# Gated delta rule heads loop: output gate read from PSUM, mask added by TensorE, lower triangle made by GpSimd

## The chip, the cores and the metric

The kernel runs on one core of a Trainium2 chip. The metric is the device time of one execution in microseconds (us), here the median of three runs. All numbers on single instructions come from one further execution that the hardware profiler recorded.

## The reference

The network has three layers on 256 tokens of width 1024: a gated delta rule (GDN) layer, a forgetting attention layer, and a block of windowed attention, pooling and an expert product over 16,384 experts. Only the GDN layer is touched. It has 8 query and key heads and 16 value heads of size 128; its projection also gives an output gate z. In the reference the chunks have 64 tokens; cut to what matters:

```python
g = cumsum(g)                                     # log decay within a chunk
decay = exp(where(lower, g[:, None] - g[None, :], -inf))
L = where(strict, (k * beta) @ k.T * decay, 0.0)
T = inverse(eye + L)                              # unit lower triangular
u, w = T @ (v * beta), T @ (k * beta * exp(g))
attn = (q @ k.T) * decay
# along the chunks
v_new = u - w @ state
o = (q * exp(g)) @ state + attn @ v_new
state = state * exp(g_last) + (k * exp(g_last - g)).T @ v_new
# behind it
o = rmsnorm(o, norm_w) * silu(z)
```

The second layer's input is scaled and shifted by a modulation vector, cond @ ada_w[1], of which the GDN layer's loop computes the first 2048 entries beside its own work.

## The kernel before, in words

Each engine has one instruction stream, written out by hand; semaphores order them against each other. No planner is used. A helper's call order in a stream is the order of its work.

The heads loop is `rounds(inner)`, eight rounds, each for one key head and its two value heads (g is 0 or 1), with the 256 tokens as two chunks of 128. Three rounds are in work at once: in round i the triangular inverse of head pair i is built (`level_p`, `mask_level`, `level_d`, `close_level`, j = 0 to 5), the pair before, f, is finished (`finish`, steps 0 to 5: values, state, second chunk, output, sum of squares), and the next pair, n, is set up. Round 0 has no f and round 7 no n. A level is a ping-pong: TensorE's product into bank PA, a masking copy by VectorE, TensorE's product into bank PB, and VectorE's subtraction from the inverse. The finish and setup products stand between the levels on TensorE in the order of `inner`.

Setup of pair n: `setup_keys` makes K K^T and K Q^T in PSUM; `setup_rows` (L2372) spreads the cumulative log decay and beta over 128 partitions into the PSUM banks ROWS; ScalarE takes EG = exp of a row (L931); VectorE adds the mask negu (`decays`, L1623) into the SBUF tile DT, ScalarE takes the exponential of DT in place (L937), VectorE multiplies beta and K K^T (`betas`, L1632) and then that and DT into the lower triangle LT (`lowers`, L1638); `setup_values` (L2393) transposes V into ROWS, and `setup_low` (L2402) gathers the diagonal blocks of LT, from which `starts` begins the next inverse. GpSimd makes the masked scores AT (L680) and the decayed queries (L683).

Output of pair f: ScalarE copies o to OS and squares it; TensorE sums the squares (L2494); ScalarE makes 1/rms (L986, L988); VectorE's `normed` multiplies OS with the norm weight and 1/rms (L1689) and then with the gate (L1692).

Modulation: SyncE loads 1 MB of ada_w[1] a round (L533), GpSimd multiplies eight slices with cond (L691) and adds them in seven additions (L696), TensorE sums over partitions with two products of one column (`modulator`, L2410), VectorE copies the result (L1696). SyncE starts the load for round i when TensorE's modulation product of round i - 2 is done; GpSimd does the slices of round i before the scores of pair i + 1.

`norm_sums` (L2356) sums squares of q and k for the pair after next. Around the loop stand the input projection before (L2253), with `setup_*` of round 0 between its last tiles, and the output projection behind it (L2551), between whose products the last `finish` stands.

## Time and profile before

| | |
|---|---|
| median of 3 runs | 1618.76 us (1617.99 to 1621.35) |
| profiled execution | 1621.4 us, its span 1619.6 us |
| TensorE (PE) busy | 1554.8 us, 96% |
| VectorE (DVE) busy | 1109.9 us, 69% |
| ScalarE (ACT) busy | 932.7 us, 58% |
| GpSimd (POOL) busy | 493.4 us, 30% |
| DMA | 255.89 MB, mean 158 GB/s |
| mean granted TensorE clock | 0.987 |

The span runs from the first to the last instruction. PE is TensorE's matmuls, PEld its weight loads, SPq SyncE's queue of DMAs. An fp32 product stands in the trace as two records, so "x4" of a shape is two products, except for transposes. A matmul's length holds a latency that overlaps the next one; the distance between starts is what it takes of the engine. "[0.67 <-PE ps L2372]" is idle time before the row and the instruction that ended it.

### The profile page before, as it was taken

The page shows a single profiled execution, that of the slowest core. Times are in us where ns is not written, and L with a number is a line of the kernel's source. Part 1 is how long each engine was busy: PE and PEld are TensorE (multiplying, and loading weights), DVE is VectorE, ACT ScalarE, POOL GpSimd, SP SyncE. Part 2 cuts the span into 40 slices and gives each one's busy share as a digit, 9 for nine tenths or more (in the row PEclk, how much of TensorE's full clock was granted, in tenths as well). Part 3 has the DMA queues.
Part 4 walks back from the last instruction along what each step waited for, and adds up shares of the span by engine and source line. Part 5 has one row for each costly group of instructions (what it writes and reads, how often), then busy time and mean ns, then how long its engine had stood idle before and what let it go on. Part 6 is the DMA issues. An engine that isn't in the chain of part 4 may idle for free.

```text
span 1619.6 us, 37025 instructions
## 1 busy us (share of the span) xinstructions
PE 1554.8 (96%) x13269; PEld 1429.3 (88%) x13269; DVE 1109.9 (69%) x2304; ACT 932.7 (58%) x1763; POOL 493.4 (30%) x405
## 2 busy tenths in 40 slices
PE   7899999899999999999999999999999999999998
PEld 6899877798998899888999999999999888888886
DVE  3787768656556653776478888798888555555554
ACT  1766567744555555545354444799898544555554
POOL 4000278661000040000067777766565100000000
PEclk9999979899999999999999999999999999999999
DMA  9668412454443344247455555544444666666663
GB/s 295 219 184 278 150 55 82 133 163 130 151 131 118 111 156 131 79 157 156 104 150 167 168 168 172 162 143 135 140 131 143 182 194 194 193 192 190 194 193 127
DMA packets 211832, 255.89 MB, mean 158 GB/s; under 512 B 15912, under 2 KB 193804, under 8 KB 211724
## 3 DMA queue, kind: packets, MB, share of 16 engines
q1 hardware_dynamic: 211723, 254.39, 53.2%
q8 instruction: 76, 1.25, 0.3%
q14 instruction: 33, 0.26, 0.1%
HBM read 253.29 MB, written 1.05 MB: 157 GB/s over the span
## 4 chain that ended last, share of the span: by engine, by line
PE 72%; DVE 11%; issue 5%; DMA 4%; ACT 4%; SPq 2%; DVEq 0%; ACTq 0%
PE ps L2253 22%; PE ps L2861 22%; PE ps L2843 10%; PE ps L2831 3%; DMA raw<-in_u_experts 3%; PE ps L2273 2%; PE ps L2551 2%; DVE raw L2014 2%; SPq L580 2%; PE ps L2628 1%; DVE w_lo L1396 1%; PE ps L2451 1%; DMA arena<-in_ada_w 1%; DVE arena L2067 1%; PE ps L2648 1%
## 5 line engine op out<-in xcount | busy, mean ns | idle before, releaser
L742 POOL TENSOR_TENSOR w_lo<-raw,w_hi 128x1024 fp32r<-128x1024 f32 x128 | 307.6, 2406 | 337.7 <-ACT w_hi L1265 337.6
L2253 PE MATMUL ps<-x_hi,w_hi 128*128 128x256 f32 x1088 | 315.3, 290 | 8.3 <-DVE w_lo L1396 3.0
L2253 PE MATMUL ps<-x_hi,w_lo 128*128 128x256 f32 x1088 | 308.2, 283 | 0.0
L2253 PE MATMUL ps<-x_lo,w_hi 128*128 128x256 f32 x1088 | 308.2, 283 | 0.0
L2212 DVE TENSOR_TENSOR w_lo<-raw,w_hi 128x1024 fp32r<-128x1024 f32 x124 | 152.0, 1226 | 143.2 <-ACT w_hi L1374 143.2
L1374 ACT ACTIVATE w_hi<-raw 128x1024 fp32r<-128x1024 f32 x124 | 131.6, 1061 | 168.0 <-PE ps L2861 168.0
L2253 PEld LDWEIGHTS ps<-x_hi,w_hi 128*128 128x128 f32 x1088 | 209.1, 192 | 15.3 <-issue 6.0
L2253 PEld LDWEIGHTS ps<-x_lo,w_hi 128*128 128x128 f32 x1088 | 209.2, 192 | 1.3 <-issue 1.2
L2253 PEld LDWEIGHTS ps<-x_hi,w_lo 128*128 128x128 f32 x1088 | 209.0, 192 | 0.0
L1265 ACT ACTIVATE w_hi<-raw 128x1024 fp32r<-128x1024 f32 x128 | 134.9, 1054 | 113.4 <-DVE raw L2014 113.2
L2806 PE MATMUL ps<-x_hi,w_hi 128*128 128x256 f32 x576 | 166.3, 289 | 10.6 <-ACT arena L1287 9.7
L2014 DVE STREAM_TRANSPOSE raw<-raw 128x1024 f32<-128x1024 f32 x128 | 158.3, 1237 | 17.1 <-DMA raw<-in_u_experts 15.8
L2806 PE MATMUL ps<-x_lo,w_hi 128*128 128x256 f32 x576 | 162.8, 283 | 0.0
L2806 PE MATMUL ps<-x_hi,w_lo 128*128 128x256 f32 x576 | 162.7, 282 | 0.0
L2861 PE MATMUL ps<-w_hi,x_hi 128*128 128x512 f32 x512 | 157.6, 389 | 1.1 <-DVE x_lo L2202 1.1
L2861 PE MATMUL ps<-w_lo,x_hi 128*128 128x512 f32 x512 | 157.7, 389 | 0.0
L2861 PE MATMUL ps<-w_hi,x_lo 128*128 128x512 f32 x512 | 157.6, 389 | 0.0
L1396 DVE TENSOR_TENSOR w_lo<-arena,w_hi 128x2048 fp32r<-128x2048 f32 (+1 forms) x43 | 97.1, 2258 | 70.0 <-ACT w_hi L759 70.0
L1396 DVE TENSOR_TENSOR w_lo<-raw,w_hi 128x2048 fp32r<-128x2048 f32 (+1 forms) x43 | 97.2, 2261 | 69.3 <-ACT w_hi L759 69.3
L2843 PE MATMUL ps<-x_lo,w_hi 128*128 128x256 f32 x448 | 131.9, 294 | 0.0
L2843 PE MATMUL ps<-x_hi,w_hi 128*128 128x256 f32 x448 | 126.7, 283 | 0.0
L2843 PE MATMUL ps<-x_hi,w_lo 128*128 128x256 f32 x448 | 126.5, 282 | 0.0
(446 smaller groups left out, 3563.7 us busy)
## 6 DMA issues: line engine op xcount, KB each, us to landing
raw<-in_u_experts SPq DMA_DIRECT2D x512, 128.0 KB, 2.7
raw<-in_v_experts SPq DMA_DIRECT2D x128, 512.0 KB, 4.3
arena<-in_ada_w SPq DMA_DIRECT2D x18, 1024.0 KB, 7.8
raw<-in_a_w_in SPq DMA_DIRECT2D x12, 1024.0 KB, 5.7
arena<-in_a_w_in SPq DMA_DIRECT2D x12, 1024.0 KB, 5.7
raw<-in_b_w_in SPq DMA_DIRECT2D x8, 1024.0 KB, 5.7
arena<-in_b_w_in SPq DMA_DIRECT2D x8, 1024.0 KB, 5.6
raw<-in_w_in SPq DMA_DIRECT2D x8, 1024.0 KB, 5.6
```

What stands on the lines that cost most here:

```text
L580: sp.dma_start(URAW[u][32 * q:32 * q + 32, :].rearrange("p (a c) -> p a c", a=4), src).then_inc(u_in[u], 16)
L742: pool.tensor_tensor(UTL[e], UT[e % 2], UTH[e].bitcast(F32), ALU.subtract).then_inc(utl_ready, 1)
L1265: act.activation(UTH[e % 4], UT[e % 2], ACT.Copy).then_inc(uth_ready, 1)
L1374: act.activation(VH[u], VRAW[u], ACT.Copy).then_inc(high_ready, 1)
L1396: v.tensor_tensor(WLO[:, slot, 0:k, :], RAW[raw_slot(base, u)][:, 0:k, :], WHI[:, slot, 0:k, :].bitcast(F32), ALU.subtract).then_inc(lo_re ...
L2014: v.transpose(UT[s_].rearrange("p (k a j) -> p a k j", k=KC, a=4), URAW[s_].rearrange("p (a k i) -> p a k i", a=4, k=KC)).then_inc(ut_read ...
L2212: v.tensor_tensor(VL[u], VRAW[u], VH[u].bitcast(F32), ALU.subtract).then_inc(low_ready, 1)
L2253: ins = mm(o[:, b * S:b * S + S], w[:, slot, kk, b * P:b * P + P], xx[:, (kk + turn) % KC, :], start=(kk == 0 and n == 0), stop=(kk == k - ...
L2806: ins = mm(ps[e % 2][:, 0:S], w[e % 4][:, kk * P:kk * P + P], xx[:, kk, :], start=(kk == 0 and n == 0), stop=(kk == KC - 1 and n == 2))
L2831: ins = mm(GB.rearrange("p (e t) -> p t e", t=4)[:, q, :], OHJ[:, c % 2, q, :], OHI[:, c % 2, q, :], start=True, stop=True, skip_group_che ...
L2843: ins = mm(ps[e % 2][:, 0:S], w[e % 4][:, kk * P:kk * P + P], xx[:, kk, :], start=m == 0, stop=m == 23)
L2861: ins = mm(ps[4 + 2 * t + h][:, :], g[:, u, t * P:t * P + P], w[u][:, 512 * h:512 * h + 512], start=False, stop=False, skip_group_check=True)
```

## The change

TensorE adds the mask negu, now bf16, to ROWS with `ident16` (`setup_masks`); `decays` goes, and ScalarE's exponential reads ROWS in PSUM and writes DT. `lowers` moves from VectorE to GpSimd, ahead of its scores. The copy of o to OS goes: VectorE's `gated` multiplies o from PSUM, the norm weight and z in place, and `normed` multiplies that with 1/rms. The modulation product moves from the end of round i to behind `setup_values` of round i + 1, has four products instead of two, and GpSimd has one addition fewer. `keep_wide` puts products of 512 bf16 columns, whose result nobody reads, ahead of some levels. The order of several steps in `inner` changes on all three engines: on TensorE `level_d(i, 1)` goes ahead of `setup_keys` and `norm_sums` ahead of `level_p(i, 5)`; on VectorE `betas` goes ahead of `close_level(i, 2)`; on ScalarE `setup_v` goes ahead of the first two `spread`.

```diff
 RNo = [temp(256)]
-negu = temp(128)
+negu = temp(64).bitcast(B16)
+temp(64)
 strict = temp(128)
...
+    def lowers(r):
+        for g in range(2):
+            pool.wait_ge(h_dt, r.nth(g, 2))
+            pool.wait_ge(h_xm, r.nth(g))
+            pool.tensor_tensor(LT[r.side][g], KKb[g], DT[g], ALU.mult).then_inc(h_lt, 1)
...
     def scores(r):
+        lowers(r)
         pool.wait_ge(g_kqs, r.count(1, 1))
...
                                ALU.mult).then_inc(mod_sum, 1)
-        for half, done in ((4, 8), (2, 12), (1, 14)):
+        for half, done in ((4, 8), (2, 12)):
             pool.wait_ge(mod_sum, 15 * i + (24 + done))
             for kk in range(half):
-                pool.tensor_tensor(w[:, kk, :], w[:, kk, :], w[:, kk + half, :], ALU.add).then_inc(mod_sum, 1)
+                pool.tensor_tensor(w[:, kk, :], w[:, kk, :], w[:, kk + half, :], ALU.add).then_inc(mod_sum, half if half == 2 and kk else 1)
         if i + 1 < GQ:
...
     def setup_decays(r):
+        if r.at:
+            act.wait_ge(h_kd, r.count(2))
+            act.wait_ge(h_at, r.count(2))
+            act.wait_ge(h_lt, r.count(2))
         for g in range(2):
...
             for cc in range(2):
-                act.activation(two(DT[g])[:, cc, :], two(DT[g])[:, cc, :], ACT.Exp,
+                act.activation(two(DT[g])[:, cc, :], ROWS[g][:, cc * 128:cc * 128 + 128], ACT.Exp,
                                bias=NGT[:, cc, r.heads[g]:r.heads[g] + 1]).then_inc(h_dt, 1)
...
-    def finish_out(r):
+    def finish_squares(r):
+        for g in range(2):
+            act.wait_ge(h_o, r.nth(g))
+            act.activation(SQo[g], A2[g], ACT.Square).then_inc(h_sq, 1)
...
+    def finish_norms(r):
         if r.at:
             act.wait_ge(h_out, r.count(2, 2))
-        for g in range(2):
-            act.wait_ge(h_o, r.nth(g))
-            act.activation(OS[g], A2[g], ACT.Copy).then_inc(h_os, 1)
-            act.activation(SQo[g], A2[g], ACT.Square).then_inc(h_sq, 1)
...
-    def finish_norms(r):
         for g in range(2):
...
         if f:
-            finish_out(f)
+            finish_squares(f)
+        if n:
+            setup_v(n)
         spread(i, 0)
         spread(i, 1)
-        if n:
-            setup_v(n)
         spread(i, 2)
...
     finish_second(Round(GQ - 1))
-    finish_out(Round(GQ - 1))
+    finish_squares(Round(GQ - 1))
     finish_norms(Round(GQ - 1))
...
-    def decays(r):
-        if r.at:
-            v.wait_ge(h_kd, r.count(2))
-            v.wait_ge(h_at, r.count(2))
-        for g in range(2):
-            v.wait_ge(h_eg, r.nth(g))
-            v.tensor_tensor(two(DT[g]), two(ROWS[g][:, 0:256]), bcast(negu, 2), ALU.add).then_inc(h_dta, 1)
...
     def keys(r):
...
         for g in range(2):
+            v.wait_ge(h_eg, r.nth(g))
             v.tensor_tensor(two(KKb[g]), two(ROWS[g][:, 256:512]), KKs, ALU.mult).then_inc(h_xm, 1)
...
-    def lowers(r):
-        for g in range(2):
-            v.wait_ge(h_dt, r.nth(g, 2))
-            v.wait_ge(h_xm, r.nth(g))
-            v.tensor_tensor(LT[r.side][g], KKb[g], DT[g], ALU.mult).then_inc(h_lt, 1)
...
-    def normed(r, g):
+    def gated(r):
         if r.at >= 6:
             v.wait_ge(z_late, 1)
+        for g in range(2):
+            v.wait_ge(h_sq, r.nth(g))
+            zb = ZB[:, r.heads[g], :]
+            v.scalar_tensor_tensor(zb, A2[g], COLS[:, CAN:CAN + 1], zb, ALU.mult, ALU.mult).then_inc(h_os, 1)
...
+    def normed(r, g):
         v.wait_ge(h_orn, r.nth(g))
         v.wait_ge(h_os, r.nth(g))
-        v.scalar_tensor_tensor(OS[g], OS[g], COLS[:, CAN:CAN + 1], RNo[g], ALU.mult, ALU.mult).then_inc(h_og, 1)
-        v.wait_ge(h_og, r.nth(g, 1, 1, 2))
         zb = ZB[:, r.heads[g], :]
-        v.tensor_tensor(zb, OS[g], zb, ALU.mult).then_inc(h_out, 1)
+        v.tensor_tensor(zb, zb, RNo[g], ALU.mult).then_inc(h_out, 1)
...
         close_level(i, 0)
+        mask_level(i, 1)
         if ahead:
             normalised_k(ahead)
-        mask_level(i, 1)
         if f and f.at:
...
             remainder(f)
-        close_level(i, 2)
         if n:
-            decays(n)
+            betas(n)
         else:
             split_x_half(1, 0, ZB[:, 0:8, :])
+        close_level(i, 2)
         mask_level(i, 3)
-        if n:
-            betas(n)
+        if n is None:
+            split_x_half(1, 1, ZB[:, 0:8, :])
         close_level(i, 3)
         mask_level(i, 4)
-        if n:
-            lowers(n)
-        else:
-            split_x_half(1, 1, ZB[:, 0:8, :])
+        if f:
+            modulator(f)
+            gated(f)
         close_level(i, 4)
...
         mask_level(i, 5)
-        modulator(i)
         if f:
...
     lo(T_AIN + 16, 0, 8)
-    decays(Round(0))
     betas(Round(0))
-    lowers(Round(0))
     v.memset(XPAIR[0:32, :, 32:64], 0.0)
...
     normed(Round(GQ - 2), 1)
+    modulator(Round(GQ - 1))
     remainder(Round(GQ - 1))
+    gated(Round(GQ - 1))
     for g in range(2):
...
         pe.wait_ge(g_norm, r.count(2, 2))
-        pe.wait_ge(ada_free, r.count(1, 9))
+        pe.wait_ge(ada_free, r.count(1, 8))
         if r.at == 0:
...
-    def setup_values(r):
+    def setup_masks(r):
         for g in range(2):
...
             pe.wait_ge(h_xm, r.nth(g))
+            for cc in range(2):
+                ins = mm(ROWS[g][:, cc * 128:cc * 128 + 128], ident16, negu, start=False, stop=True, skip_group_check=True)
+            ins.then_inc(h_dta, 1)
...
+    def setup_values(r):
+        for g in range(2):
+            pe.wait_ge(h_dt, r.nth(g, 2))
             for cc in range(2):
...
         for cc in range(2):
-            ins = mm(MODP[:, cc:cc + 1], RAW[MOD_SLOT[r.side]][:, 0, cc * 128:cc * 128 + 128], ones[:, 0:1], start=True, stop=True)
+            for half in range(2):
+                ins = mm(MODP[:, cc:cc + 1], RAW[MOD_SLOT[r.side]][:, half, cc * 128:cc * 128 + 128], ones[:, 0:1],
+                         start=(half == 0), stop=(half == 1))
         ins.then_inc(raw_free, 1)
...
-    def level_p(r, j):
+    def keep_wide(bank_, n):
+        for _ in range(n):
+            mm(bank_[:, :], ident16, BG3, start=True, stop=True)
...
+    def level_p(r, j, spare=0):
         lt = LT[r.side]
+        keep_wide(PA, spare)
         if j == 0:
...
-    def level_d(r, j):
+    def level_d(r, j, spare=0):
+        if j == 0 and r.at:
+            pe.wait_ge(h_xx, r.count(12))
+        keep_wide(PB, spare)
         pe.wait_ge(h_pm, r.count(6, j + 1))
...
             pe.wait_ge(h_xt, r.count(3, 3))
-            if r.at:
-                pe.wait_ge(h_xx, r.count(12))
         elif j < 5:
...
             elif step == 3:
-                pe.wait_ge(h_og, r.nth(g, 1, 0, 2))
+                pe.wait_ge(h_og, r.nth(g))
                 mm(B2[g][:, 128:256], INVT[r.side][:, 2 * g + 1, :], R1[g], start=True, stop=True).then_inc(h_s3, 1)
...
                 pe.wait_ge(h_sq, r.nth(g))
+                pe.wait_ge(h_os, r.nth(g))
                 mm(B2[g], ones, SQo[g], start=True, stop=True).then_inc(h_oss, 1)
...
         level_p(i, 0)
-        level_d(i, 0)
+        level_d(i, 0, 2)
         if f:
             finish(f, 0)
-        level_p(i, 1)
+        level_p(i, 1, 0 if f else 2)
         if f:
             finish(f, 1)
+        level_d(i, 1, 0 if f else 2)
         if n:
             setup_keys(n)
-        level_d(i, 1)
+        level_p(i, 2, 0 if n else 1)
         if f:
             finish(f, 2)
-        level_p(i, 2)
         if n:
             setup_rows(n)
-        level_d(i, 2)
+        level_d(i, 2, 0 if n else 1)
         if f:
             finish(f, 3)
+        if n:
+            setup_masks(n)
         level_p(i, 3)
...
             finish(f, 4)
-        level_d(i, 3)
+        level_d(i, 3, 0 if f else 2)
         if n:
             setup_values(n)
-        level_p(i, 4)
-        level_d(i, 4)
+        if f:
+            modulator(f)
+        level_p(i, 4, 0 if n else 2)
+        level_d(i, 4, 1)
         if f:
...
             setup_low(n)
-        level_p(i, 5)
-        modulator(i)
         if i.at + 2 < GQ:
             norm_sums(Round(i.at + 2))
+        level_p(i, 5, 0 if f else 2)
         level_d(i, 5)
...
     pe.wait_ge(cv_out, 16)
+    setup_masks(Round(0))
     setup_values(Round(0))
...
         finish(Round(GQ - 1), step)
+        if step == 1:
+            modulator(Round(GQ - 1))
     for u in range(1, 4):
         pe.wait_ge(lo_ready, tile_no(T_AOUT, 0, u))
+        if u == 2:
+            pe.wait_ge(ada_free, 10 + GQ)
         if u < 3:
...
         else:
```

## Rows read from the trace of the kernel before

**Rows 1.** The page, part 4: shares of the last chain by engine.

```profile
PE 72%; DVE 11%; issue 5%; DMA 4%; ACT 4%; SPq 2%; DVEq 0%; ACTq 0%
```

**Rows 2.** By stretch: us, busy (count) of each engine, granted clock, DMA share, GB/s.

```profile
196.30:203.30 7.00, 4.80 (x235) 3.56 (x235) 3.73 (x15) 2.12 (x9) 6.84 (x12) 0.99 0.02 5
203.30:220.30 17.00, 15.33 (x277) 12.07 (x278) 8.16 (x24) 7.63 (x26) 14.15 (x22) 0.50 0.21 64
...
230.90:246.20 15.30, 14.36 (x401) 11.21 (x400) 13.02 (x38) 11.77 (x39) 13.15 (x20) 1.00 0.22 71
...
309.10:322.70 13.60, 11.95 (x252) 10.14 (x252) 5.62 (x17) 7.64 (x15) 6.26 (x9) 0.50 0.76 241
```

**Rows 3.** Timeline of round 2, TensorE: start, length, engine, line, shapes, count.

```profile
230.86 0.45 PE L2424 MATMUL ps<-arena 32*32 32x32 f32 x32
...
233.84 0.61 PE L2381 MATMUL ps<-arena 128*128 128x128 f32 x4
...
234.94 0.44 PE L2451 MATMUL ps<-arena 32*32 32x16 f32 x32
...
236.39 0.60 PE L2372 MATMUL ps<-arena,small 128*128 128x512 bf16 x2
...
238.32 0.49 PE L2489 MATMUL ps<-arena 128*128 128x128 f32 x2
...
240.23 0.66 PE L2393 MATMUL ps<-small,arena 128*128 128x128 f32 x4
...
240.81 0.44 PE L2429 MATMUL ps<-arena 32*32 32x32 f32 x16
...
242.03 1.13 PE L2494 MATMUL ps<-arena,small 128*128 128x256 f32 x4
...
243.09 0.45 PE L2402 MATMUL ps<-small,arena 32*32 32x32 f32 x32
...
244.07 0.61 PE L2410 MATMUL ps<-small,arena 128*128 128x1 f32 x4
...
244.54 1.10 PE L2356 MATMUL ps<-arena,small 128*128 128x512 f32 x2
...
245.58 0.67 PE L2462 MATMUL ps<-arena 64*64 64x64 f32 x8
...
246.18 0.45 PE L2424 MATMUL ps<-arena 32*32 32x32 f32 x32
```

**Rows 4.** Timeline of round 2, ScalarE and VectorE.

```profile
236.88 0.45 ACT L931 ACTIVATE arena<-ps 128x128 f32<-128x128 f32 x2 [0.67 <-PE ps L2372]
...
237.44 0.22 DVE L1664 TENSOR_TENSOR arena<-arena,ps 128x64 f32<-128x64 f32 x1 [0.22 <-PE ps L2451]
...
241.51 1.25 DVE L1638 TENSOR_TENSOR arena<-arena 128x256 f32<-128x256 f32 x2
...
244.90 0.43 DVE L1658 COPY arena<-ps 64x256 f32<-64x256 f32 x1
```

**Rows 5.** Timeline of GpSimd, rounds 1 and 2, and the landing of L533's DMAs.

```profile
232.46 5.69 POOL L696 TENSOR_TENSOR arena<-arena 128x256 f32<-128x256 f32 x7
...
240.06 1.41 POOL L680 TENSOR_TENSOR arena<-arena 128x256 f32<-128x256 f32 x2 [1.92 <-PE ps L2491]
...
242.44 4.69 POOL L691 TENSOR_TENSOR raw<-raw,small 128x256 f32<-128x256 f32 x7
...
DMA to landing us min/median/max: 5.0/5.3/7.8
```

**Rows 6.** Timeline, TensorE: projection's end, start of rounds 1 and 7, last finish.

```profile
194.10 0.60 PE L2393 MATMUL ps<-small,arena 128*128 128x128 f32 x4
...
213.03 0.65 PE L2424 MATMUL ps<-arena 32*32 32x32 f32 x32
...
308.42 0.45 PE L2424 MATMUL ps<-arena 32*32 32x32 f32 x32
...
327.95 0.69 PE L2474 MATMUL ps<-arena 128*128 128x128 f32 x4 [0.86 <-issue]
```

## The prediction

> **What bounds the kernel now.** I read the page's chain of waits first: 72% of the span is TensorE, so what counts is TensorE's order of work [rows 1]. Only the heads loop, between 196 and 328 us, and its two neighbours are edited, so the next view is the busy time and granted clock by stretch. Two stretches, 17.0 and 13.6 us long, were granted 0.50 of the clock, which is the 1.2 GHz level; both come just after stretches in which TensorE had many short pauses (before the first, 4.80 us busy of 7.00). A steady round has the full 2.4 GHz and TensorE 14.36 us busy of 15.30 [rows 2]. The third view is TensorE's timeline of one steady round: from the first level product (230.86) to the next round's (246.18) it takes 15.32 us [rows 3]. Start-to-start distances there are the prices of blocks of products. VectorE, ScalarE and GpSimd are read beside it [rows 4, 5].
>
> In such a round the chain alternates between TensorE (level products) and VectorE (masks, closings). At 235 TensorE does the key products ahead of the level-1 product. Around 238.3 it does the twelve output passes (L2489 to L2491) ahead of the level-3 closing product. From 241.5 VectorE does the two lower-triangle products, 1.25 us, and only then closes level 4. From 243.1 to 246.2 TensorE is all but closed up: 0.98 for the low blocks and level 5, 0.47 for the modulation product, 1.04 for the norm sums, 0.60 for the closing [rows 3, 4].
>
> **The change, part by part, in a steady round.** I count from the first level product as 0.
>
> *Start.* Two wide products stand before the level-0 closing. One wide bf16 product costs 0.21 (two of the same shape, L2372, show 0.60 with 0.2 of latency in it [rows 3]), so 0.43. They start only after VectorE's last closing, which comes at about 0.55, so the closing product starts at about 1.05, where it now starts at about 1.0. Cost 0.1.
>
> *Level 1.* The key products move behind the level-1 closing product. They take 1.1 (233.84 to 234.94 [rows 3]), and VectorE's late output gate is one operation instead of two (0.7 less). Level 1 closes 0.65 earlier, at 3.95. The keys then end at 4.45, and the row products start at about 5.3 instead of 5.53.
>
> *Betas.* They now stand before the level-2 closing on VectorE, and wait for ScalarE's exponentials, which start 0.49 after the row products (236.39 to 236.88 [rows 3, 4]). So the first beta starts at 6.1 and the second ends at 6.85; level 2 closes at 6.9, where it closed at 6.58 (237.44 [rows 4]). The 0.65 is gone and 0.3 more. The removed decay additions (two VectorE operations, some 0.7) give that back before the level-3 mask, which stays at 7.7.
>
> *Mask by TensorE.* Four bf16 products of 128 columns, a quarter of a wide one each: 0.2 with a wait for the betas until 7.0. The bounds are 0 (hidden in that wait) and 0.6 (priced as the transposes of L2393 [rows 3]); I take 0.15 on the path. The output passes run from 7.6 to 9.14 (now 7.46 to 9.0, since they wait for ScalarE's copy).
>
> *Modulation product behind the values.* It has four products instead of two. Two take 0.47 (244.07 to 244.54), so four take 0.94. The value transposes take 0.58 (240.23 to 240.81 [rows 3]). Today the level-4 product follows these transposes at once, at 9.95. In the new order it waits for 9.51 + 0.58 + 0.94 = 11.03: **1.1 us on the path**. This is the largest single step. Its lower bound is 0, if the matrix unit overlapped the extra loads; its upper bound 1.1. I take the upper one, since the row is of the very same instruction.
>
> *Lower triangle to GpSimd, output gate from PSUM.* VectorE loses 1.25 between the level-4 mask and its closing and gains the two gate products. No row shows a gate read from PSUM at 256 columns. Its nearest rows are one operation of the present lower product (0.63, both inputs in SBUF [rows 4]) and the copy of a level from PSUM (0.43, L1658 [rows 4]); I take 0.4 each, and 0.1 for the modulation copy: 0.9 against 1.25, a gain of 0.3. Level 4 closes at 12.75 (now 11.93).
>
> *Tail.* The output sums on TensorE now wait for each gate product; from the last one at 12.98 come 0.53 (half of 242.03 to 243.09), low blocks and level 5 with 0.98 and, between them now, norm sums with 1.04: level 5 ends at 15.53 [rows 3]. Then VectorE's level-5 copy (0.43, 15.63 to 16.06) and, 0.2 later, the closing product with 0.60: next round at 16.85. Today the modulation and norm products stand between level 5 and its closing, where they hide the copy. **The round grows from 15.32 to 16.85, by 1.5.**
>
> *GpSimd.* Today: score products and decayed queries 2.38 (240.06 to 242.44), eight modulation products some 5.3 (seven take 4.69), seven sums 5.69 [rows 5]. New: one sum fewer (-0.8) and two lower products (+1.4, as the 1.41 of the two score products): 14.0 in 16.85, not the bound. The DMA of the next modulation weights now starts only behind the moved product, at 11.2; it lands 5.3 later [rows 5], at 16.5, so GpSimd works from about -0.3 to 9.8 and has the lower triangle at 11.2, wanted by the low blocks at 13.5. The cover is 2.3 us.
>
> The Trainium skill, "GPSIMD Engine Reference", section "Engine selection", gives two-input elementwise work on GpSimd as about twice as slow as on VectorE. The trace does not show that factor: 0.70 each on GpSimd [rows 5] against 0.63 on VectorE [rows 4]. By the rule the two would be about 1.1 us dearer, which the cover takes in steady rounds and which would be added once, in round 0.
>
> **The other rounds.** *Lead-in and round 0.* The mask products stand behind the input projection, which ends at 194.10 [rows 6]. The decay exponentials, two a head of the shape that takes 0.45 a pair in the row, 0.65 a pair with the second input's wait (my estimate) [rows 4], then end at 195.0 and 195.65, GpSimd's lower products at 196.5. GpSimd's own turn binds round 0: from 195.05 scores and so on take 14.0, the next lower products end at 210.4, and low blocks, norm sums, two wide products, level 5, copy and closing, priced as above, make 214.2. Today 213.03 [rows 6]: +1.2. *Round 1* is a steady one at full clock if the wide products hold the clock: 16.85 against 230.86 - 213.03 = 17.83: -1.0. *Rounds 2 to 5* +1.5 each: +6.0; a pause of 1.3 us without a cause in the view, in one of them, is left as it is. *Round 6* has no norm sums, so VectorE's copy and not TensorE sets its tail: 16.4 against 15.3: +1.1. *Round 7* takes 19.53 now (308.42 to 327.95 [rows 6]), 13.6 of it at half clock. TensorE was busy 11.95 us in that stretch [rows 2], so full clock gives back 6 at most (half) and 0 at least, where VectorE's and ScalarE's waits fill in. With four blocks of the round before between the levels 0.5 shorter each, the output passes 1.4 shorter (half of what they would take at 0.50) and eight level products 0.2 shorter each, the gain is 2.0 + 1.4 + 1.6 = 5.0; the modulation product and the wide products, now on the path, take 0.9 and 0.7 of it: -3.4. *Behind the loop* the last modulation product stands between output products: +0.9.
>
> Sum: 1.2 - 1.0 + 6.0 + 1.1 - 3.4 + 0.9 = **+4.8 us**. The profiled execution took 1621.4 (span 1619.6 and 1.8 around it); the median of the three runs is 2.6 lower, 1618.76. With the same offset the forecast is 1623.6.
>
> **The rivals.**
> - *The clock falls again* in rounds 0 to 1 and 7 in spite of the wide products: eleven in round 0, but only three in a round like 1 and seven in round 7, of 0.2 us each. For it: after stretches with many pauses both falls came; against: steady rounds with 14.36 of 15.30 busy stay at 2.4 GHz [rows 2]. The gains of 3.4 and 1.0 go, and about 1 more is lost in round 0: +10, 1629. 
> - *TensorE's additions fall into its waits.* Rounds 2 to 6 stay at 15.3: 4.8 less 7.1 is -2.3, 1616.5; round 1 would be shorter by 1.5 too, 1615. It decides if the level-4 product can start before 10.1. For it: TensorE's busy share counts overlapped ends; against: the rows of the block distances.
> - *VectorE's relief comes through* (the other side). VectorE loses some 2.5 us of 13.0 a round; if the level chain, and not TensorE's order, sets the rounds, each of six ends 1 us earlier than now: -2.3 - 6 = -8.3, 1610.5. It decides if norm sums and modulation overlap VectorE's part. Against it: the tail from 243.1 is closed up on TensorE.
> - *The weights come late to GpSimd*, since their DMA starts behind the moved product. It decides if landing takes over 5.3 + 2.3 = 7.6 us; one took 7.8. Then some 0.5 a round more: 1627.
>
> **How the numbers follow.** Forecast 0.50 (its own range 1620 to 1628), clock falls 0.12, additions hidden 0.20, relief comes through 0.15, late weights 0.03. A change under 0.2% (3.2 us) can't be told from none here. Faster: all of the relief, half of the hidden case and an edge of the forecast's, 0.27. Same: the other half and a fifth of the forecast, 0.20. Slower: 0.53. The range takes in the mask and modulation bounds and most of both sides: 1611 to 1630.
>
> **What would show it.** Right: steady rounds of 16.5 to 17 us; a level-4 product some 1.5 us behind the value transposes with eight modulation records between; norm sums closing up before level 5; no stretch at 0.50 in the loop; round 7 near 16. Wrong: rounds of 15.3 or less, a granted clock of 0.50 around 205 or 315, or GpSimd waiting for a DMA before its modulation products and TensorE's low blocks waiting for GpSimd.

## The result, and the profile after

| | before | after |
|---|---|---|
| median of 6 runs, us | 1618.38 (1616.18 to 1621.35) | 1630.38 (1622.19 to 1639.23) |
| mean granted clock of the runs | 0.987 (profiled) | 0.982 to 0.995, median 0.9895 |
| profiled execution (span), us | 1621.4 (1619.6) | 1639.23 (1637.5) |

The changed kernel is slower: ratio 1.0076, interval 1.0042 to 1.0111, 12.0 us between the medians. The forecast was 1623.6, with 1620 to 1628 as its own range and 1611 to 1630 as the whole; 1630.4 lies just outside. The direction was right, the size was not: +12 where +4.8 was forecast.

The runs of the changed kernel lie 17 us apart, and they follow the granted clock: 1622.19 us at 0.995, 1629.44 to 1630.99 at 0.988 to 0.991, 1637.45 at 0.985, 1639.23 at 0.982. That is 17.0 us for 0.013 of mean clock. The profiled one is the slowest, so its rows show more of the fall than the median does. In the middle runs the mean clock is not lower than in the kernel before: what is missing against the forecast is not a fall below the old clock but the gain that the forecast took for granted, as is worked out below.

Busy time by round of the changed kernel, from its profiled execution (stretch, length; PE, PEld, DVE, ACT, POOL busy and count; granted clock; DMA share; GB/s). The rows of before with which to compare them are [rows 2]:

```profile
197.90:205.90 8.00, 6.97 (x174) 4.72 (x177) 2.69 (x10) 1.16 (x4) 7.90 (x14) 0.57 0.01 2
214.50:234.30 19.80, 18.34 (x410) 14.68 (x412) 10.05 (x32) 11.17 (x36) 10.42 (x17) 0.83 0.17 56
234.30:251.70 17.40, 15.68 (x407) 12.21 (x409) 10.49 (x33) 11.41 (x37) 12.98 (x21) 1.00 0.21 65
251.70:268.70 17.00, 15.52 (x407) 12.24 (x408) 10.47 (x33) 11.33 (x38) 13.01 (x21) 1.00 0.20 65
268.70:288.70 20.00, 18.48 (x407) 14.70 (x408) 10.79 (x33) 11.47 (x38) 13.00 (x21) 0.83 0.17 56
305.75:323.60 17.85, 16.34 (x405) 13.36 (x406) 10.36 (x33) 11.33 (x36) 14.15 (x23) 0.86 0.30 99
323.60:347.20 23.60, 21.52 (x357) 16.73 (x360) 10.07 (x29) 11.64 (x23) 7.84 (x12) 0.50 0.47 152
```

A round at full clock now takes 17.0 us instead of 15.3 (DVE went from 13.02 to 10.47, as planned). Rounds 1 and 4 have a stretch at the 1.2 GHz level and take 19.8 and 20.0; round 7 runs at 0.50 from end to end. The stretches by themselves:

```profile
199.20:206.00 6.80, 5.93 (x121) 3.88 (x115) 1.94 (x7) 1.16 (x4) 6.64 (x12) 0.51 0.01 2
216.30:223.10 6.80, 6.80 (x117) 5.84 (x118) 2.23 (x9) 2.27 (x8) 4.57 (x7) 0.52 0.02 6
...
270.90:277.70 6.80, 6.71 (x116) 5.60 (x116) 3.36 (x10) 2.27 (x8) 6.64 (x10) 0.51 0.02 6
...
318.70:356.20 37.50, 34.82 (x451) 28.89 (x454) 16.07 (x41) 16.97 (x36) 9.24 (x14) 0.50 0.43 140
```

Together 57.9 us at half clock where [rows 2] have 17.0 + 13.6. The last one starts in round 6's tail and goes on 9 us into the output products behind the loop.

TensorE in a steady round at full clock (round 3, from 251.69; start, length, engine, line, shapes, count), the answer to [rows 3]:

```profile
251.69 0.45 PE L2438 MATMUL ps<-arena 32*32 32x32 f32 x32
...
252.50 0.38 PE L2424 MATMUL ps<-arena,small 128*128 128x512 bf16 x1 [0.35 <-DVE arena L1672]
252.81 0.44 PE L2466 MATMUL ps<-arena 32*32 32x16 f32 x32
...
257.99 0.44 PE L2466 MATMUL ps<-arena 32*32 32x16 f32 x32
...
258.90 0.58 PE L2393 MATMUL ps<-arena,small 128*128 128x128 bf16 x4
259.42 0.45 PE L2438 MATMUL ps<-arena 32*32 32x32 f32 x32
259.80 0.49 PE L2504 MATMUL ps<-arena 128*128 128x128 f32 x2
...
261.71 0.66 PE L2400 MATMUL ps<-small,arena 128*128 128x128 f32 x4
262.20 0.95 PE L2418 MATMUL ps<-small,arena 128*128 128x1 f32 x8
263.08 0.44 PE L2443 MATMUL ps<-arena 32*32 32x32 f32 x16
264.46 1.10 PE L2510 MATMUL ps<-arena,small 128*128 128x256 f32 x4
265.49 0.45 PE L2409 MATMUL ps<-small,arena 32*32 32x32 f32 x32
265.88 1.13 PE L2356 MATMUL ps<-arena,small 128*128 128x512 f32 x2
266.93 0.68 PE L2448 MATMUL ps<-arena 64*64 64x64 f32 x8
268.13 0.68 PE L2477 MATMUL ps<-arena 64*64 64x64 f32 x8 [0.52 <-DVE arena L1656]
268.74 0.45 PE L2438 MATMUL ps<-arena 32*32 32x32 f32 x32
```

L2438 is a level product, L2424 a wide one, L2466 a level closing, L2393 the masks, L2504 the output passes, L2400 the values, L2418 the modulation product, L2443 level 4, L2510 the output sums, L2409 the low blocks, L2356 the norm sums, L2448 and L2477 level 5. The round takes 17.05 us.

VectorE and GpSimd in the same round, the answers to [rows 4, 5]:

```profile
251.25 5.26 POOL L699 TENSOR_TENSOR raw<-raw,small 128x256 f32<-128x256 f32 x8 [4.26 <-DMA raw<-in_ada_w]
...
255.96 0.21 DVE L1662 TENSOR_TENSOR arena<-arena,ps 128x64 f32<-128x64 f32 x1
...
258.32 0.75 DVE L1636 TENSOR_TENSOR arena<-ps,arena 128x256 f32<-128x256 f32 x2 [0.27 <-ACT arena L939]
258.99 0.21 DVE L1662 TENSOR_TENSOR arena<-arena,ps 128x64 f32<-128x64 f32 x1
...
260.81 1.42 POOL L679 TENSOR_TENSOR arena<-arena 128x256 f32<-128x256 f32 x2
...
263.84 0.86 DVE L1688 SCALAR_TENSOR_TENSOR arena<-ps,small,arena 128x256 f32<-128x256 f32 x2
...
267.65 0.43 DVE L1656 COPY arena<-ps 64x256 f32<-64x256 f32 x1 [0.59 <-PE ps L2448]
```

L679 is the lower triangle on GpSimd, L1636 the betas, L1662 the closing of levels 1 and 2, L1688 the gate from PSUM, L1656 the level-5 copy.

Where the time went, first level product to first level product, both profiled executions:

| | before | after | more | forecast |
|---|---|---|---|---|
| lead-in and round 0 | to 213.03 | to 214.45 | +1.4 | +1.2 |
| round 1 | 17.83 | 19.83 | +2.0 | -1.0 |
| rounds 2 to 5 | 62.48 | 71.47 | +9.0 | +6.0 |
| round 6 | 15.08 | 17.88 | +2.8 | +1.1 |
| round 7 | 19.53 | 23.60 | +4.1 | -3.4 |
| behind it, to the last output product | 51.70 | 55.86 | +4.2 | +0.9 |
| rest of the span | 1239.95 | 1234.41 | -5.5 | 0 |
| span | 1619.6 | 1637.5 | +17.9 | +4.8 |

The last output products start at 379.65 and 403.09. What stands behind them is edited in no kernel here, and it took 1234.4 to 1240.0 us in the fourteen profiled executions; its -5.5 is scatter, and it hides that up to there the changed kernel's profiled execution is 23.4 us behind. Kernels are therefore compared by medians and ratios, and single executions up to a row of the loop.

### The profile page after: what moved, and what is told of

It is laid out like the page before. It is cut to its first block, busy times and chain, and to the rows that moved or that the text cites. A ratio compares the mean times of both kernels' runs of the same rounds, so it can differ in the third digit from the quotient of the medians.

```text
span 1637.5 us, 37191 instructions
## 1 busy us (share of the span) xinstructions
PE 1573.1 (96%) x13341; PEld 1444.2 (88%) x13369; DVE 1090.5 (67%) x2272; ACT 928.7 (57%) x1747; POOL 492.1 (30%) x413
## 3 DMA queue, kind: packets, MB, share of 16 engines
HBM read 253.29 MB, written 1.05 MB: 155 GB/s over the span
## 4 chain that ended last, share of the span: by engine, by line
PE 64%; issue 19%; POOL 10%; DVE 3%; ACT 3%; SPq 0%; DMA 0%; POOLq 0%; another core or an unknown queue 0%; DVEq 0%; ACTq 0%
PE ps L2885 21%; PE ps L2253 14%; PE ps L2867 9%; POOL w_lo L750 8%; PE ps L2855 3%; PE ps L2571 2%; PE ps L2273 1%; PE ps L2466 1%; PE ps L2300 1%; PE ps L2652 1%; PE ps L2438 1%; PE ps L2510 1%; PE ps L2418 0%; POOL arena L740 0%; ACT w_hi L767 0%
```

## The experiments

Two theories. **Order:** the longer steady round, as forecast, makes the time. **Clock:** the new order lets the granted clock fall more often, in spite of the wide products, and this is more than half of the 12 us. Each experiment ran beside the kernel before on the same chip. The median of the kernel before was 1621.9 to 1622.9 there, and 1618.38 beside the changed kernel, so between kernels the ratios are compared, not the microseconds. The steady round is read from one or two rounds at full clock of the profiled execution.

| kernel | median us (n) | ratio to before, interval | mean clock | steady round |
|---|---|---|---|---|
| after | 1630.38 (6) | 1.0076, 1.0042 to 1.0111 | 0.982 to 0.995 | 17.05 |
| e1_no_wide | 1654.88 (5) | 1.0193, 1.0176 to 1.0210 | 0.966 to 0.972 | |
| e2_before_wide | 1622.82 (11) | 1.0001, 0.9992 to 1.0011 | 0.986 to 0.992 | 15.85 |
| e3_mod_back | 1630.53 (7) | 1.0050, 1.0036 to 1.0063 | 0.981 to 0.990 | 16.75 |
| e4_norm_back | 1633.99 (7) | 1.0059, 1.0036 to 1.0082 | 0.980 to 0.994 | 16.54 |
| e5_more_wide | 1627.57 (12) | 1.0037, 1.0023 to 1.0050 | 0.989 to 0.997 | 17.04 |
| e6_two_products | 1631.28 (6) | 1.0054, 1.0037 to 1.0070 | 0.987 to 0.989 | 16.58 |
| e8_wide_ends | 1621.33 (12) | 0.9993, 0.9979 to 1.0007 | 0.987 to 0.995 | 15.33 |
| e9_mod_moved | 1634.05 (6) | 1.0069, 1.0048 to 1.0090 | 0.974 to 0.982 | 15.60 |
| e10_before_filled | 1619.69 (12) | 0.9979, 0.9969 to 0.9990 | 0.993 to 0.998 | 15.33 |
| e11_lower_gpsimd | 1626.21 (10) | 1.0017, 1.0008 to 1.0026 | 0.983 to 0.987 | 15.54 |
| e12_lower_gate | 1622.82 (10) | 1.0003, 0.9994 to 1.0012 | 0.981 to 0.987 | 15.25 |
| e13_moved_wide | 1632.70 (4) | 1.0070, 1.0053 to 1.0086 | 0.980 to 0.986 | 15.9 |

The kernel before had 0.984 to 0.990 in these runs.

**The changed kernel without its wide products.**

```diff
             def keep_wide(bank_, n):
-                for _ in range(n):
+                for _ in range(0):
```

> The changed kernel without any of its wide products (nothing else edited). In its profile the steady round takes 17.05 us (15.3 before), and TensorE has half clock for 58 us around the loop (30.7 before), so two theories share the loss of 12 us. Theory A: the wide products hold the clock up, imperfectly; without them rounds 0, 1 and 7 lose it at least as in the kernel before and steady rounds more often: half clock over 40 us in the profile, time 1630 to 1640. Theory B: the clock falls because the longer rounds have more pauses, and the few wide products hardly matter: half clock as with them (30 to 60 us), steady round 17.0, time within 3 us of the changed kernel's 1630. Theory C: they do harm: time under 1626.

A ratio of 1.0193 where the changed kernel has 1.0076: some 20 us slower. The wide products work, more than any of the three theories expected (theory A had 1630 to 1640). Stretches of its profile (columns as above):

```profile
198.80:229.50 30.70, 27.02 (x592) 20.21 (x592) 13.72 (x43) 11.12 (x37) 22.65 (x37) 0.50 0.01 3
253.40:267.10 13.70, 12.79 (x210) 9.72 (x201) 6.96 (x19) 5.17 (x15) 9.52 (x14) 0.51 0.13 44
273.90:291.00 17.10, 16.18 (x253) 11.63 (x257) 8.69 (x23) 6.76 (x21) 9.29 (x14) 0.51 0.19 62
```

The clock falls again and again in the middle rounds, where the kernel before never has it below full ([rows 2], 230.9). 102.4 us near the loop are at half clock. So the new order without wide products makes the clock fall (0.966 to 0.972), and with them it comes back to about the clock of the kernel before (median 0.9895 against 0.987), at best to 0.995.

**The kernel before with the same wide products.** The edit is `keep_wide` and the counts of the change, at the same places.

> The kernel before with the same numbers of wide products at the same levels, nothing else. Theory A: round 0 (11 of them) and round 7 (7 of them) keep the full clock, half clock under 12 us instead of 30.7; steady rounds 15.4 (0.1 longer); time 4 to 6 us under the kernel before, 1612 to 1614. Theory B: half clock stays near 30 us; time 1618 to 1620.

Missed: no gain. The clock rose (mostly 0.991), but each steady round took 15.85 instead of 15.3. The rows of one round, from its level product at 249.82:

```profile
249.82 0.45 PE L2429 MATMUL ps<-arena 32*32 32x32 f32 x32
250.23 0.41 DVE L1674 TENSOR_SCALAR arena<-ps 64x256 f32<-64x256 f32 x1
250.69 0.60 PE L2415 MATMUL ps<-arena,small 128*128 128x512 bf16 x2 [0.42 <-DVE arena L1674]
251.23 0.44 PE L2457 MATMUL ps<-arena 32*32 32x16 f32 x32
```

The level-0 closing product starts 1.41 after the level product; in the kernel before it is 1.00. The two wide products wait for VectorE's last closing and then stand in the way. I had put 0.1 on this step. Half clock did not fall under 12 us either: the profiled execution, the one with the lowest clock (0.986), has 34 us of it near the loop.

**Wide products only where there are pauses.** First in rounds 0 and 7 alone, then in every pause of the lead-in and of rounds 0, 6 and 7, none in rounds 1 to 5. The core of the second edit, on the kernel before:

```diff
+                level_d(i, 0, 0 if f and n else 2)
...
+                if n is None:
+                    keep_wide(PB, 3)
...
+                if f is None or i.at + 2 >= GQ:
+                    pe.wait_ge(h_xx, i.count(12, 11))
+                    keep_wide(PB, 2 if f is None else 3)
             setup_keys(Round(0))
...
+            keep_wide(PA, 4)
```

> The kernel before with the wide products only in round 0 and round 7. In all rounds they raised the mean clock from 0.987 to 0.991 and cost 0.55 us in each steady round (15.85 against 15.3), mostly because the first two wait behind VectorE's last closing. Here: steady round 15.3, mean clock 0.990 to 0.992, so 1617 to 1619 against 1621.9 for the kernel before in the same session (0.15 to 0.3% faster). Rival: the gain of clock came from the steady rounds: clock 0.987, no difference.

> The kernel before with wide products wherever TensorE pauses in the lead-in and in rounds 0, 6 and 7 (also ahead of the last closing product, the output-copy wait of round 7 and the level-3 product of round 0), none in rounds 1 to 5. With those in rounds 0 and 7 alone the mean clock was 0.987 to 0.995 and half clock fell near 205 to 212 and 314 us. Theory A (pauses decide): mean clock 0.993 to 0.997 in most runs, steady round 15.3, median 1614 to 1618, so 0.3% or more under the kernel before and under both kernels. Theory D (falls come at random whatever fills the pauses): clock 0.987 to 0.992 and 1620 to 1622.

The first made no difference (ratio 0.9993), with the clock nearly as expected (median 0.990) and without the 0.15% or more that was expected of it. The second is 0.2% faster than the kernel before, the only version here that is; its clock was as theory A had it (0.993 to 0.998), its time, 1619.69, above the 1614 to 1618. Its stretches:

```profile
198.00:209.30 11.30, 9.91 (x302) 6.46 (x302) 7.41 (x25) 5.71 (x20) 11.06 (x18) 1.00 0.02 4
209.30:212.70 3.40, 3.40 (x24) 1.41 (x27) 0.20 (x2) 1.85 (x4) 3.32 (x7) 0.52 0.68 217
227.80:244.03 16.23, 14.55 (x400) 11.40 (x398) 13.06 (x38) 11.81 (x39) 13.19 (x20) 1.00 0.21 70
244.03:259.37 15.34, 14.35 (x400) 11.26 (x398) 13.06 (x38) 11.80 (x39) 13.18 (x20) 1.00 0.23 71
309.00:318.50 9.50, 7.18 (x191) 5.16 (x190) 4.60 (x13) 4.57 (x13) 3.21 (x5) 1.00 0.73 233
318.50:332.20 13.70, 13.14 (x90) 9.44 (x89) 7.40 (x14) 5.98 (x14) 0.00 (x0) 0.51 0.01 3
```

Half clock near the loop is 17.1 us instead of 30.6, and the steady round is unchanged (15.34). At the price of a busy round (0.43 us for each us at half clock, worked out below) the 13.5 us fewer would be 5.8; the median is 3.2 shorter. The rounds of this profiled execution show where it comes and goes. Round 7 starts at

```profile
305.26 0.45 PE L2429 MATMUL ps<-arena 32*32 32x32 f32 x32
```

where it was 308.42 before [rows 6]: 3.2 ahead, of which 2.6 come from round 1, which is at full clock now (15.25 instead of 17.83). Round 7 then takes 23.2 us instead of 19.5, with about the same 13.7 at half clock: TensorE pauses for 1.82 us in the middle of a closing product, until 317.77, a pause for which the trace names no wait, and of the wide products behind it three take 1.42 at half clock (322.11 to 323.53). So round 7 had no more of the full clock than before; the 5.0 that I had taken for it is shown by no run.

**The changed kernel with more wide products.** Two ahead of each round's last closing product, where TensorE waits 0.52 for VectorE's copy, and nine in the lead-in:

```diff
+                pe.wait_ge(h_xx, i.count(12, 11))
+                keep_wide(PB, 2)
                 level_d(i, 5)
```

> The changed kernel with more wide products: two ahead of the last closing product of every round (TensorE waits 0.5 us there for VectorE's copy), and nine in the lead-in between projection and round 0. The kernel without any of them had the full clock least (0.966 to 0.972 mean, 1655 us), the changed one 0.982 to 0.995. Theory A (the clock follows how closed up TensorE is, and run-to-run spread is the spread of the falls): mean clock 0.992 to 0.996 in all runs, time 1622 to 1626, spread under 5 us, steady round 17.0 to 17.2. Theory D (the falls are random, wide products have done what they can): clock 0.982 to 0.995 and 1622 to 1639 as before.

```profile
210.00:330.00 120.00, 109.85 (x2750) 84.42 (x2772) 70.42 (x218) 76.34 (x231) 88.81 (x138) 0.97 0.26 82
```
```profile
314.94 0.45 PE L2438 MATMUL ps<-arena 32*32 32x32 f32 x32
324.08 0.50 PE L2466 MATMUL ps<-arena 32*32 32x16 f32 x20 [2.78 <-issue]
```

Its profiled execution, 1624.5 us at 0.996, has 6.8 us at half clock near the loop instead of 57.9, and the same round of 17.04. Eight of twelve runs were at 0.994 to 0.997 with 1624.4 to 1628.8 us; four at 0.989 to 0.991 with 1629.7 to 1634.1. So theory A is right in the mean and not in all runs: the spread is 9.8 us, where it had under 5. The wide products in the pause cost nothing. The median stands 5 to 6 us above the kernel before.

That is not yet the price of the order, since the kernel before runs at 0.987. The kernel before with its pauses filled is the fair partner (median clock 0.996, here 0.9955): ratio 1.0037 against 0.9979, some 9 us. The profiled executions say the same. In the loop both are at full clock up to round 7, but for 3.4 us in round 0 of the filled one, and round 7 starts at 314.94 here and at 305.26 there: 9.7 us. The forecast's terms of the order up to round 7 are 1.2 + 1.5 + 6.0 + 1.1 = 9.8 (1.5 for round 1 is a steady round's growth). Rounds 1 and 6, at full clock here, take 17.02 and 16.39, forecast 16.85 and 16.4. Round 7, with 6.8 us at half clock and a pause of 2.78 us that again no wait explains (324.08 above), takes 21.0; what it takes at full clock no run shows.

**Parts of the order, undone in the changed kernel.** Two modulation products with a seventh sum on GpSimd; the modulation product back at its round's end; the norm sums back behind level 5:

```diff
-                    for half in range(2):
-                        ins = mm(MODP[:, cc:cc + 1], RAW[MOD_SLOT[r.side]][:, half, cc * 128:cc * 128 + 128], ones[:, 0:1],
-                                 start=(half == 0), stop=(half == 1))
+                    ins = mm(MODP[:, cc:cc + 1], RAW[MOD_SLOT[r.side]][:, 0, cc * 128:cc * 128 + 128], ones[:, 0:1], start=True, stop=True)
```
```diff
-                if f:
-                    modulator(f)
                 level_p(i, 4, 0 if n else 2)
...
+                modulator(i)
                 level_d(i, 5)
```
```diff
+                level_p(i, 5, 0 if f else 2)
                 if i.at + 2 < GQ:
                     norm_sums(Round(i.at + 2))
-                level_p(i, 5, 0 if f else 2)
```

> The changed kernel with the modulation product of two parts and GpSimd's seventh addition restored; its place stays. By distances (0.47 less on TensorE ahead of the level-4 product) the steady round is 16.6 instead of 17.05; GpSimd's 0.8 more is covered. At equal clock 3 us less. Rival: no change in the round, since VectorE's gate sets the next step.

> The changed kernel with the modulation product (all four of them) back at the end of its own round, on TensorE and VectorE. By my block distances the level-4 product starts 0.95 earlier, the product then takes 0.94 between level 5 and its closing, where 0.35 of it is hidden behind the level-5 copy: steady round 16.45 instead of 17.05, GpSimd no longer waits 4 us for the DMA; at equal clock 4 us less in all (7 rounds of 0.6). Rival (the place is free, the order of the rest makes the round long): steady round 17.0, within 1 us.

> The changed kernel with the norm sums back behind the level-5 product. By my block distances level 5 ends 1.04 earlier, VectorE's start steps then set the copy and the closing product 0.35 earlier: steady round 16.7 instead of 17.05, 2 us in all at equal clock. Rival: the chain runs through VectorE alone, no change in the round.

The first kept its round as expected: 17.05 to 16.58. Its rows of values, modulation and level 4:

```profile
280.34 0.66 PE L2400 MATMUL ps<-small,arena 128*128 128x128 f32 x4
280.83 0.50 PE L2417 MATMUL ps<-small,raw 128*128 128x1 f32 x4
281.26 0.44 PE L2441 MATMUL ps<-arena 32*32 32x32 f32 x16
```

Level 4 starts 0.43 behind the modulation product, where it is 0.88 in the changed kernel (262.20 to 263.08): four records fewer, 0.45 less, all of it on the path. The second gained half of what was expected (0.3), the third 0.5, 0.15 more than expected, each read from one round; another round at full clock took 17.52 and 16.97 there. In time all three lie a little under the changed kernel (1.0054, 1.0050 and 1.0059 against 1.0076) and inside its interval (1.0042 to 1.0111), so gains of 2 to 4 us are neither shown nor ruled out: at clocks of 0.981 to 0.990 and 0.980 to 0.994 the fall decides more than 0.3 or 0.5 a round.

**Parts of the change, alone in the kernel before.** The modulation product moved behind the values, in four products (the hunks of the change that concern it); the lower triangle on GpSimd; that and the gate from PSUM:

```diff
                 if n:
                     setup_values(n)
+                if f:
+                    modulator(f)
                 level_p(i, 4)
...
-                modulator(i)
```
```diff
             def scores(r):
+                lowers(r)
```

> The kernel before with one part of the change alone: the modulation product, in four parts, behind the value transposes of the next round, and one GpSimd addition fewer. No wide products. By distances the level-4 product starts 0.94 later; the tail loses the 0.47 of the two products, but is set by VectorE's copy: steady round 16.1 instead of 15.3, GpSimd waits 4 us a round for its DMA, 6 us in all at equal clock. If pauses decide the clock, the mean clock falls to 0.98 or less and the time passes 1635. Rival: the product fits a pause, 15.3 and 1622.

> The kernel before with one part alone: GpSimd makes the lower triangle ahead of its scores, VectorE no longer does. The level-4 closing comes 0.5 earlier, but behind the output sums TensorE is closed up to the next round: steady round 15.2 to 15.3 by my distances (the 1.25 us on VectorE is not what sets it), time within 2 us of before at equal clock. Rival (VectorE's chain sets the round): steady round 14.6 to 14.9, 3 to 5 us faster.

> As the one with the lower triangle on GpSimd, and the output gate from PSUM (ScalarE's copies go, VectorE's gate comes behind the level-4 mask, the output sums wait for it). By my distances the gate costs 0.8 between mask and closing and lets the output sums start 0.2 later: steady round 15.4 to 15.5, 1 us slower than the other in all. Rival: ScalarE's and VectorE's relief makes it 15.0 or less.

With the modulation product moved and made of four, and one GpSimd addition fewer, the kernel is about as slow as with the whole change (1.0069 against 1.0076), though its steady round grows by 0.3 us only, where 0.8 was expected:

```profile
230.00:245.60 15.60, 14.46 (x401) 11.67 (x401) 11.66 (x37) 11.71 (x39) 11.94 (x18) 0.99 0.22 72
245.60:259.30 13.70, 13.35 (x202) 9.88 (x201) 7.72 (x22) 6.14 (x17) 9.94 (x14) 0.51 0.21 73
269.90:285.50 15.60, 14.50 (x405) 11.73 (x406) 12.05 (x38) 11.80 (x39) 12.22 (x18) 1.00 0.23 71
313.90:331.00 17.10, 15.08 (x306) 12.47 (x305) 9.89 (x26) 10.03 (x19) 10.29 (x17) 0.51 0.73 239
334.40:348.10 13.70, 12.62 (x65) 11.71 (x64) 6.41 (x13) 4.44 (x9) 0.00 (x0) 0.51 0.20 67
```

It has 64.9 us at half clock near the loop, where the kernel before has 30.6. Of the 11.6 us between the medians its steady rounds explain 5 x 0.3; the other 10 go with the clock (0.974 to 0.982), about what was expected if pauses decide it (0.98 or less, over 1635). Late weights are not the reason: GpSimd waits for their DMA, but no row of TensorE in the loop waits for GpSimd. It has no wide products, so this is to be held against the changed kernel without them (1.0193) rather than against the changed one. The rule of the Trainium skill, "TensorE: Matmul & The Clock Gate", section "Part 1: The HAM clock gate", that the rate follows how busy the array has lately been, is borne out by the runs without and with more wide products; but the busy share of a whole round does not tell which one is followed by a fall: 14.46 of 15.60 in the row just before the fall at 245.6 here, and 14.55 of 16.23 in round 2 of the filled one (227.80), which keeps the full clock.

GpSimd's lower triangle alone costs 0.2 a round and some 3 us in all; expected were rounds of 15.2 to 15.3. With the gate from PSUM the rounds at full clock take 15.25 and 15.46 and the time is as before (1.0003), where 1 us more than with the triangle alone was expected: these two parts of the change pay for each other and bring nothing.

**The moved product with two wide ones ahead of the last closing.**

> The kernel before with the modulation product moved, as measured (steady round 15.6, but mean clock 0.974 to 0.982 and 1634 us), and two wide products ahead of the last closing product of each round, where the modulation product stood. If its 12 us come from the clock and the clock from the pause that the move opened there: mean clock at least 0.987, 1622 to 1626, steady round 15.6 to 15.8. Rival (the loss is order or DMA, not clock): 1630 or more with the clock up.

Missed: the clock came back only to 0.980 to 0.986, the round grew to 15.9, the time stayed (1.0070, four runs). So the pause ahead of the last closing is not what alone makes this kernel fall; which one does is open.

**The two theories, weighed.** Order, its wide products included: between kernels of nearly the same clock it costs 9 to 10 us (1.0037 against 0.9979). Clock: it decides where in the 17 us a run of the changed kernel ends. That falls make more than half of the 12 us between the medians is not borne out, since the median run of the changed kernel has no lower clock than the kernel before; they are why the gain by a held clock, which would have paid for half of the order, did not come.

## Why the prediction was wrong, point by point

- *Start, 0.1:* the level-0 closing came at 1.12 (1.05 forecast). Right here; in the kernel before the same products cost 0.4.
- *Level 1, betas* (starts of the rows): VectorE closed level 1 at 4.27 (3.95 forecast), began the betas at 6.63 (6.1) and closed level 2 at 7.30 (6.9). The direction of each step was right; half a us of lateness had gathered by here.
- *Masks, 0.15:* mis-sized. 258.90 to 259.42 is 0.52 on the path, near the upper bound of 0.6 that I had from the transposes. I had priced them by their columns, as quarters of a wide product, and the rows charge them nearly as the transposes. The output passes start at 8.11, forecast 7.6. The masks were not tried alone.
- *Modulation product, 1.1:* right. Level 4 at 11.39 (11.03 forecast), the 0.36 being about the masks' excess of 0.37. The block itself took 0.88, the forecast 0.94, and the halved one gave back 0.47 of a round. That it was all on the path holds inside the changed kernel; alone in the kernel before it cost 0.3, as two products' 0.47 at the tail is saved at the same time.
- *Lower triangle and gate, 0.3 gained:* small, as forecast. The gates took 0.43 each (0.4 forecast). Alone in the kernel before, the two together changed a round by -0.1 to +0.15.
- *Tail:* norm sums at 14.19 (13.9), level 5 at 15.24 (14.9), its closing at 16.44, next round at 17.05 (16.85). The copy that norm and modulation products used to hide now shows as a 0.52 wait, as forecast.
- *GpSimd:* the weights' DMA starts late and L699 waits 4.26 for it, but the lower triangle ends at 262.23, 3.3 ahead of the low blocks. Not the bound, as forecast.
- *The whole steady round:* +1.75 instead of +1.5.
- **The step that failed:** "Round 1 is a steady one at full clock if the wide products hold the clock", -1.0, and in round 7 "full clock gives back", -3.4 with the additions taken off. The wide products did not hold the clock in most runs (median 0.9895, before 0.987). Without this gain the forecast's own terms give 4.8 + 2.5 (round 1, +1.5 instead of -1.0) + 5.0 (round 7, +1.6 instead of -3.4) = 12.3, and 12.0 was measured between the medians; that they meet so closely is partly luck, as the clock of a median run is not that of the kernel before to the last us. The one run at 0.995 took 1622.19, 3.8 above the kernel before: about the forecast.
- *The profiled execution,* the slowest, shows falls where the sum had none besides: 6.8 us in round 4 (19.96 instead of 17.05, +2.9), the tail of round 6 (17.88 instead of the 16.39 at full clock, +1.5), the first 9 us of the output products (55.0 us from the first to the last instead of 51.3). Each us at half clock in a busy round costs 2.9 / 6.8 = 0.43. Rounds 1 and 7 came 3.0 and 7.5 above the forecast; with round 4 they make 13.4 of the 13.1 by which the profiled span missed it. That the rest adds up to nothing is chance: the falls in round 6 and in the output products are made up by the 5.5 of scatter behind the last output product.
- *The signs:* of the signs of being wrong, "a granted clock of 0.50 around 205 or 315" came (199.2 to 206.0, and from 318.7); of those of being right, the steady round, the eight modulation records and the norm sums.
- *The rivals:* the one that came true is "the clock falls again", 1629, to which I gave 0.12. Its price was nearly right, partly by luck: it counted the lost gains as 4.4 where the forecast's own terms make them 7.5, added about 1 in round 0, and did not see that falls come in round 4, in round 6 and behind the loop too. What I held against it, that steady rounds with 14.36 of 15.30 busy stay at 2.4 GHz, was a row of the old order and did not carry over. Additions hidden: refuted by the 17.05. VectorE's relief: refuted, DVE lost 2.55 us a round and the round grew. Late weights: the landing stayed in its cover.

What stays open: what decides in a given execution whether the clock falls, since runs of one and the same kernel lie 0.013 apart; why output products without pauses (8.97 of 9.00 us busy) ran at half clock until 356.2; which pause it is that the moved modulation product makes worse; and what the pauses of 1 to 3 us in the middle of a block are, for which no wait stands in the trace. The two named above (ending at 317.77 and 324.08) lie right beside the start of a fall (318.5 and 323.2), but one of 1.13 us in the kernel before (ending at 251.72) is followed by none, and the falls of the changed kernel have no such pause before them.

## What to carry to other kernels

Price TensorE's granted clock as a term of its own when its order of work changes: read it per run, and give it a range as wide as its falls (here 17 us, more than any term of the sum). A working by block distances gave the steady round to within 0.5 us in every kernel here and the order's cost up to round 7 to 0.1 us (9.8 for 9.7), but it says nothing about the clock. Filler products belong only in front of a wait that TensorE has anyway: ahead of the copy of level 5 they were free, ahead of the level-0 closing of the kernel before they cost 0.4 us a round and ate what they brought.

## What the runs showed that was not expected

- One small product moved (0.88 us of TensorE's time, where it was 0.47) cost 11.6 us of 1622, and only 1.5 of these are in the length of the steady rounds.
- Products that compute nothing, some 0.2 us each, made a kernel some 20 us faster (ratio to the kernel before 1.0193 without, 1.0076 with them).
- Two-input elementwise work on GpSimd is hardly slower than on VectorE here: 1.42 for two 128x256 products (L679) against 1.25 on VectorE [rows 4].
